# The first block's Down projection as seven block products, with a changed entry and norm around it

## What is computed

```python
# first_block, end
x = x + mix @ w_out[l]
h = rms_norm(x, g_ffn[l])
x = x + (jax.nn.silu(h @ w_gate[l]) * (h @ w_up[l])) @ w_down[l]   # D_FF = 2816
# second_block, start: 16 meta tokens stand ahead of x
u = rms_norm_2(h, g_mix[layer])
z = jnp.einsum('bld,df->blf', u, w_in[layer])
```

## Time and profile before

| | us |
|---|---|
| median of 3 runs | 3392.05 (3387.78 to 3392.68) |
| the profiled execution, device time | 3388.14 |
| its span, first to last instruction | 3386.3 |
| PE busy, PEld busy | 3217.8 (95%), 2841.0 (84%) |
| DVE, ACT, POOL busy | 1649.5 (49%), 1126.6 (33%), 992.5 (29%) |
| mean granted TensorE clock | 0.975 |

### The profile page before, as it was taken

The page is one execution under the profiler, slowest core; times in us unless marked ns, Lnnn a source line. Parts: engine busy times, 40 slices in busy tenths (PEclk is TensorE's granted clock), DMA queues, the critical chain, the costliest instruction groups (busy, mean ns, idle before and its releaser), DMA issues.

```text
span 3386.3 us, 51779 instructions
## 1 busy us (share of the span) xinstructions
PE 3217.8 (95%) x20325; PEld 2841.0 (84%) x20325; DVE 1649.5 (49%) x2795; ACT 1126.6 (33%) x2100; POOL 992.5 (29%) x672
## 2 busy tenths in 40 slices
PE   7999989899999998999999899999999999789997
PEld 5677767688887887999999799998999999679997
DVE  4555556655554545666666723255455044522223
ACT  3433333333322213555555621155455111300002
POOL 3112223787772323222222133200000222012222
PEclk9999999999999998999999999999999999889998
DMA  4011112122234112000000012100000121468988
GB/s 155 26 32 32 32 63 87 63 87 75 81 107 173 45 45 93 20 20 26 20 20 20 14 44 82 65 25 26 23 23 20 69 95 62 175 216 308 318 307 292
DMA packets 80577, 294.90 MB, mean 87 GB/s; under 512 B 11298, under 2 KB 16226, under 8 KB 77200
## 3 DMA queue, kind: packets, MB, share of 16 engines
q1 hardware_dynamic: 69744, 251.92, 21.2%
q0 software_dynamic: 6160, 18.63, 2.2%
q10 hardware_dynamic: 4496, 21.90, 1.6%
HBM read 239.39 MB, written 47.70 MB: 85 GB/s over the span
## 4 chain that ended last, share of the span: by engine, by line
PE 55%; DVE 3%; issue 2%; ACT 1%; DMA 0%; POOL 0%; POOLq 0%; SPq 0%; DVEq 0%; ACTq 0%
PE PS L630 14%; PE PS L3003 7%; PE PS L3425 7%; PE PS L618 5%; PE PS L3188 4%; PE PS L3455 3%; PE PS L3067 3%; PE PS L3034 3%; PE PS L3264 3%; PE PS L3229 2%; PE PS L3068 0%; PE PS L3016 0%; PE PS L3201 0%; DVE where L2855 0%; PE PS L3265 0%
## 5 line engine op out<-in xcount | busy, mean ns | idle before, releaser
L652 POOL CAST w_hi<-ring 128x1024 fp32r<-128x1024 f32 x130 | 137.9, 1061 | 1547.8 <-PE PS L630 436.0
L654 POOL TENSOR_TENSOR w_lo<-ring,w_hi 128x1024 fp32r<-128x1024 f32 x130 | 333.2, 2563 | 10.5
L2142 ACT ACTIVATE EA<-EA,small_sb 128x1040 f32<-128x1040 f32 x144 | 166.8, 1158 | 192.5 <-DVE small_sb L2545 192.2
L2545 DVE CUSTOM_DVE_ANT_0 EA<-PS,biasH,low_a 128x1024 f32<-128x1024 f32 x128 | 163.5, 1278 | 56.4 <-PE PS L3034 56.4
L3003 PE MATMUL PS<-u_hi,w_hi 128*128 128x348 f32 x504 | 173.5, 344 | 0.0
L3003 PE MATMUL PS<-u_lo,w_hi 128*128 128x348 f32 x504 | 162.1, 322 | 0.0
L3003 PE MATMUL PS<-u_hi,w_lo 128*128 128x348 f32 x504 | 161.9, 321 | 0.0
L1563 DVE TENSOR_TENSOR hid_lo<-hid,hid_hi 128x1024 fp32r<-128x1024 f32 x44 | 95.0, 2200 | 121.7 <-ACT hid_hi L1213 121.7
L1647 PE MATMUL PS<-u_hi,w_hi 128*128 128x512 f32 x352 | 147.2, 418 | 3.0 <-POOL w_lo L654 2.3
L630 PE MATMUL PS<-u_hi,w_hi 128*128 128x348 f32 (+1 forms) x552 | 131.2, 342 | 13.1 <-POOL w_lo L654 7.4
L3067 PE MATMUL PS<-Va,PTa 128*128 128x128 f32 (+1 forms) x1152 | 139.9, 275 | 0.0
(11 more groups left out here) (479 smaller groups left out, 8260.2 us busy)
## 6 DMA issues: line engine op xcount, KB each, us to landing
ring<-in_stream SPq DMA_DIRECT2D x130, 512.0 KB, 3.5
w_gate_sb<-in_w_gate SPq DMA_DIRECT2D x64, 512.0 KB, 6.6
w_up_sb<-in_w_up SPq DMA_DIRECT2D x64, 512.0 KB, 7.0
w_down_sb<-in_w_down SPq DMA_DIRECT2D x64, 512.0 KB, 5.7
gu_raw<-in_gate_up SPq DMA_DIRECT2D x22, 1024.0 KB, 5.6
hid_keep<-hid_out SPq DMA_DIRECT2D x17, 512.0 KB, 2.9
hid<-hid_keep SPq DMA_DIRECT2D x17, 512.0 KB, 10.4
x_keep<-xT ACTq DMA_DIRECT2D x1, 4176.0 KB, 13.0
```

The lines of the kernel that those rows point to most:

```text
L652: pool.tensor_copy(w_hi[j][:, :, :], w_raw[j][:, :, :]).then_inc(S["w_rounded"], 1)
L654: pool.tensor_tensor(w_lo[j][:, :, :], w_raw[j][:, :, :], w_hi[j][:, :, :], ALU.subtract).then_inc(S["w_split"], 1)
L2142: act.activation(e[0:m, :], e[0:m, :], ACT.Exp, scale=-1.0, bias=small[0:m, 8 + 2 * par + k:9 + 2 * par + k], accum_out=small[0:m, 12 + 2 ...
L2545: dve.tensor_tensor_reduce(e[0:m, 0:T1], wide(2 * k, T1, m), bias, -1.0, low_a[0:m, t, k:k + 1], ALU.add, ALU.min, low).then_inc(S["aa_max ...
```

## The change

1. **Down by seven block products.** The weights are cut into 2x2 blocks (11 hidden chunks by 4 output chunks), the hidden values into 2x2 blocks (11 hidden chunks by 512 tokens). Seven products s0 to s6 (DP1, DP2, DP7, DP5, DP6, DP3, DP4) of 11 steps each make 77 steps `q`; one step has 4 output chunks x 3 passes = 12 matmuls of 512 columns, 924 in all where there were 1056. In each step ACT rounds the weights (`d_hi`) and the values (`o_hi`), POOL makes `d_lo` and DVE `o_lo`; there are four buffers of each.
2. **Operands made step by step.** The weights' sums: S3 by DVE (for s2), S1, S2, S4 by POOL (for s3, s4, s5), one step ahead. The values' differences T1, T3, T2, T4 by DVE, in steps of s0, s1, s3, s4, written over `hid`. Each product is added to one to four places of `x2T` by DVE in the steps of the next product.
3. **Loads.** Raw blocks of 256 KB come to 12 slots by SP, 99 of them. ACT issues 15 of the 17 reloads of hidden chunks. Chunks 0 and 1 are stored and reloaded, 2 to 5 stay. Early in gate and up, `gu_raw1` waits for two stores and 8 lo parts only; its roundings stand between those of t4.
4. **Norms.** In the entry of gate and up root, reciprocal and diagonal stand earlier, and the spreading stands before A22, in banks 2 and 3. At the end of Down the squares' sums go straight through a 128x128 matrix of ones; root and reciprocal are taken of 128x1044 values in SBUF (`sd2`).
5. **Splits.** The second block's tiles A0 and A0+1 are both split by POOL within Down's last product.

```diff
+KH = NF // 2
+DOWN = (("A11", "B11"), ("A12", "B21"), ("S3", "T3"), ("S1", "T1"), ("S2", "T2"), ("S4", "B22"), ("A22", "T4"))
+RAW_SLOTS = 12
+STEP_SLOTS = 4
+TWIST = 4
+ADDS = (2, 1, 1, 1, 2, 1, 1)
...
         def norm_total(dve, k):
+            if k == 2:
+                for n, cols in enumerate((slice(0, BANK), slice(BANK, TP))):
+                    dve.wait_ge(N["sd"], pieces_upto(1) + n + 1)
+                    dve.reciprocal(sd2[:, cols], sd2[:, cols]).then_inc(N["r"], 2)
+                dve.wait_ge(N["r"], 2 * pieces_upto(2))
+                return
...
-            return dve.scalar_tensor_tensor(dst, src[:, c, 0:width], gains[:, NORM_GAINS[k] + c:NORM_GAINS[k] + c + 1], wide(8 - pieces[k] - 1, width),
+            root = sd2[:, 0:width] if k == 2 else wide(8 - pieces[k] - 1, width)
+            return dve.scalar_tensor_tensor(dst, src[:, c, 0:width], gains[:, NORM_GAINS[k] + c:NORM_GAINS[k] + c + 1], root,
...
@@ SP
-                sp.wait_ge(S["keep_st"], 16 + 16 * KD)
-                sp.wait_ge(S["op_lo"], 7 * HALF)
+                sp.wait_ge(S["x_st"], 32)
+                sp.wait_ge(S["op_lo"], 8)
                 load_pair(1)
...
+                for f in range(STAY.start):
+                    sp.dma_start(hid[:, f, :], hid_keep[:, f, :]).then_inc(S["hid_ld0"], 16)
+                for n in range(4, len(RAWS)):
+                    load_down(n)
...
@@ POOL
+                for q in range(DSTEPS):
+                    if q + 1 < DSTEPS:
+                        combine_down(q + 1)
+                    pool.wait_ge(S["dw_hi"], q + 1)
+                    pool.tensor_tensor(d_lo[q % STEP_SLOTS][:, :], weight_source(q), d_hi[q % STEP_SLOTS][:, :], ALU.subtract).then_inc(S["dw_lo"], 1)
+                    if q == DP4 * KH + 5:
+                        pool.wait_ge(S["dw_lo"], DP4 * KH + 1)
+                        split(pool, A0, 0, A0 // 2 + 1, A0 - 2)
+                    if q == DP4 * KH + 8:
+                        split(pool, A0 + 1, 1, A0 // 2 + 1, A0 - 1)
...
@@ ACT
                 for q in range(HALF):
                     act.wait_ge(S["op_t"], 3 * HALF + 2 * q + 2)
                     round_operand(t4, q, t4_raw[q % 2][:, :])
+                    round_slot(1, (A11, S1, S2, S3)[q])
...
+                load_hid(STAY.stop, 11)
+                act.wait_ge(S["gs_used"], used(NF - 1, S1))
+                load_hid(11, 15)
...
                 act.dma_start(x2T[:, :, :], x_keep).then_inc(S["keep_ld"], 16)
...
+                for q in range(STEP_SLOTS, DSTEPS):
+                    if q == STAY.stop:
+                        act.wait_ge(S["hid_ld"], 16 * (NF - 1 - STAY.stop))
+                    round_weight(q)
+                    round_values(q)
...
+                for n, (cols, sums) in enumerate(((slice(0, BANK), bank(5)), (slice(BANK, TP), wide(6, TP - BANK)))):
+                    act.wait_ge(N["ss"], 4 + n)
+                    act.activation(sd2[:, cols], sums, ACT.Sqrt, scale=1.0 / D, bias=eps[:, :]).then_inc(N["sd"], 1)
...
@@ DVE
-                first_sums(0)
+                norm_recip(dve, 1)
+                for all_tokens in tiles_of(1):
+                    diagonals(dve, sq[0], by_token(1), all_tokens).then_inc(N["r"], 1)
                 for q in range(HALF):
                     lower_operand(b22, q, right(xm, HALF + q), 5 * HALF + q + 1, mix_gain(HALF + q))
-                up_right(0)
+                first_sums(0)
...
+                for k in range(2):
+                    combine_values(DP1, k)
+                dve.wait_ge(S["keep_ld"], 32)
+                for q in range(2, DSTEPS):
+                    s, k = divmod(q, KH)
+                    rest_values(q)
+                    if q + 1 < DSTEPS:
+                        combine_weights(q + 1)
+                    combine_values(s, k)
+                    p, late = divmod(k - 3, 2)
+                    if s and p >= 0 and not late:
+                        add_product(s - 1, p)
...
@@ PE
+                for q in range(DSTEPS - TWIST):
+                    operands_ready(q)
+                    for p in range(HALF):
+                        last = down_step(q // KH, q % KH, p)
+                    last.then_inc(S["dn_used"], 1)
+                operands_ready(DSTEPS - 1)
+                for p in range(HALF):
+                    for k in range(KH - TWIST, KH):
+                        last = down_step(DP4, k, p)
+                last.then_inc(S["dn_used"], 1)
+                pe.wait_ge(N["acc"], 2 * (KD + 1) + CREDIT)
+                mm(bank(5), ones[:, :], acc[:, 0:BANK], start=True, stop=True).then_inc(N["ss"], 1)
+                mm(bank(6), ones[:, :], acc[:, BANK:T1], start=True, stop=True)
+                mm(bank(7, TP - T1), ones[:, :], acc[:, T1:TP], start=True, stop=True).then_inc(N["ss"], 1)
```

More of the change, by code:

```diff
@@ L53 @@
 EVICT = "v s c22 w u1 c11 g0 c12 g1 hid1 c21 u0 hid0".split()
-KEPT = 4
+STAY = range(2, 6)
+KH = NF // 2
+DOWN = (("A11", "B11"), ("A12", "B21"), ("S3", "T3"), ("S1", "T1"), ("S2", "T2"), ("S4", "B22"), ("A22", "T4"))
+DSTEPS = KH * len(DOWN)
+RAW_OF = {"A11": ("A11",), "A12": ("A12",), "A22": ("A22",), "S3": ("A11", "A21"), "S1": ("A21", "A22"), "S2": ("A11",), "S4": ("A12",)}
+RAWS = [(s * KH + k, name, k) for s, (w, _) in enumerate(DOWN) for k in range(KH) for name in RAW_OF[w]]
+RAW_SLOTS = 12
+STEP_SLOTS = 4
+TWIST = 4
+DP1, DP2, DP7, DP5, DP6, DP3, DP4 = range(7)
+ADDS = (2, 1, 1, 1, 2, 1, 1)
 HEADS = 8
@@ L474, in build @@
         S.update(first_sems)
+        dw_lds = [nc.alloc_semaphore(name=f"dw_ld{j}") for j in range(RAW_SLOTS)]
         xin_lds = [sem(f"xin_ld{j}") for j in range(NT)]
@@ L1199, in _ @@
                         take_first(i)
-                    for s in (A11, S1, S2, S3, A12):
+                    for s in (A11, S1, S2, S3, A12) if i else (A12,):
                         round_slot(i + 1, s)
@@ L1206, in _, with load_hid @@
                 take_first(NF - 1)
-                silu_half(NF - 1, 0)
-                def round_tile(m, c):
-                    act.wait_ge(S["w_used"], tile_done(DOWN0 + m - 2))
-                    for k in range(2):
-                        act.activation(hid_hi[2 * slot + k][:, :], hid[:, bass.ds(c + k, 1), :].rearrange("p a n -> p (a n)"), ACT.Copy).then_inc(S["hid_hi"], 1)
+                def load_hid(first, last):
+                    for f in range(first, last):
+                        act.dma_start(hid[:, f, :], hid_keep[:, f, :]).then_inc(S["hid_ld"], 16)
@@ L1538, in _ @@
                     diagonals(dve, sq[0], by_token(1), all_tokens).then_inc(N["r"], 1)
+                for q in range(HALF):
+                    lower_operand(b22, q, right(xm, HALF + q), 5 * HALF + q + 1, mix_gain(HALF + q))
+                first_sums(0)
+                dve.wait_ge(S["gs_used"], used(0, S3))
+                evict(0, "s", c21[:, :], product_bank(0, S3), v_sum[:, :], ALU.add, "v")
                 for q in range(HALF):
@@ new lines, in down_step @@
+                def down_step(s, k, p):
+                    j = (s * KH + k) % STEP_SLOTS
+                    if k == 0:
+                        if s == 0 and p:
+                            pe.wait_ge(S["gs_out"], out_of(NF - 1, "w"))
+                        if s >= 2:
+                            pe.wait_ge(S["dn_ev"], added(s - 2, p))
+                    for q, (w, src) in enumerate(((d_hi, o_hi), (d_hi, o_lo), (d_lo, o_hi))):
+                        last = mm(down_bank(s, p), w[j][:, p * P:(p + 1) * P], src[j][:, :], start=(k == 0 and q == 0), stop=(k == KH - 1 and q == 2))
+                    if k == KH - 1 and p < HALF - 1:
+                        last.then_inc(S["dn_p"], 1)
+                    return last
@@ L3509, in layout @@
     late += [*w_in2[GB:GB + KD], *w_b, *w_out2]
-    out["stream"] = np.concatenate([np.stack(tiles), down, np.stack(late)])
+    out["stream"] = np.concatenate([np.stack(tiles), np.stack(late)])
     for n in ("w_gate_2", "w_up_2"):
```

341 lines of the change are left out of this document (199 added, 142 removed).

## The result

The changed kernel is slower: 3406.83 us in the median (3404.97 to 3407.66) where the kernel before has 3392.05 (five runs of each, the latter 3386.54 to 3392.68); the ratio is 1.0048, with a 95% interval of 1.0034 to 1.0061. The prediction was 3387.3 with a range of 3370 to 3403, so the time lies above the range, on the side that I held less likely.

The account below looks back on a forecast made before the run. Matmuls times their distance plus PE's holes bound gate and up and Down; -7.5 (entry), +1.2 (Down) and +1.5 (norm) make -4.8 us on the profiled 3388.1, and with 3.9 for the median 3387.3, range 3370 to 3403.

Parts of the forecast that it names:

- What bounds the kernel: In gate and up and Down, time is matmuls times their distance, 0.2267 us each in Down, plus PE's holes.
- PE's own work: Down falls from 1056 to 924 matmuls, 29.9 us less; one step of 12 is 2.72 us.
- The arrival of x2T: Down's start: DVE's rest of step 2 waits for x2T until 1046; a hole of some 17 us, 1.65 of slow clock.
- DVE and POOL exclude each other: Down's steps: turns cost 3.42 us per step in s3 and s4, 2.96 in s5; together 13.2 us, bounds 5 and 20.
- s2 has the same with S3 in place of a difference: Down's s2: one POOL and two DVE instructions per step, 2.2 us, under PE's 2.72.
- the three steps ahead are used up first: Down's s3 and s4: the lead is spent before PE lags, so step 54's operands are 10.6 us late.
- Down's end: Before the last four steps: POOL's split brings 3.3 us of waiting, perhaps a low clock; 3.9 us, bounds 2 and 6.
- The entry: Entry of gate and up: the second hole goes, the second chunk starts at 608.5; -7.5 us, bounds -5 and -10.
- A22 still ends at about 608.5: Entry of gate and up: DVE gets to t4 at about 599.4, 599.6 before, so A22's end stays at about 608.5.
- The norm: After Down: -0.8 earlier product, +6.5 for reading SBUF, -3.5 for the early split, -0.7 low clock; +1.5 us, bounds -3 and +5.
- The rivals: Whole kernel: faster one 3373, chance 0.28; slower one 3398 or 3402, 0.27; one below 3355, 3 in 100.
- B, the slower one: Down's s3 and s4: steps cost 3.9 us instead of 3.42, +10.6, 3398, or 3402 with a falling clock; chance 0.27.

Follow-up runs that it names:

- all edits: The changed kernel with the six edits, the old norm, S1, S2 and S4 summed by DVE, and TWIST = 2: 3349.79 us, ratio 0.9878.
- TWIST = 2: The kernel with the six edits and the old norm, only Down's last 2 steps, not 4, run output chunk by output chunk: 3358.62 us.
- the six edits: Changed kernel with x2T waited for at step 14, S3 ahead of the rest, A0+1 split later, chunk 1 roundings behind t4, two reorderings at Down's start: 3367.55 us.

## Why the prediction was wrong

**What bounds the kernel, and PE's own work** were right: 12 matmuls take 2.72 us wherever PE is fed, and with all edits Down is 30.6 us shorter than before. That this is so near to 29.9 is chance: it still has 6.1 us of waiting and slow clock, and Down before had 6.8.

**The arrival of x2T.** Right: the wait, what is queued behind it, and that it costs about 20 us. The term was mis-sized by 3.1 us. I took 1046 as the landing, 21.8 us after the issue, out of a sum of 15.8 MB; it took 24.5. The step that failed is "as the raw blocks are on the other queue", by which I left out the up to 1.6 MB of six more raw blocks: 14 had been issued and 17.35 MB moved by the landing, which is the upper end, 1050, of my own sum. The slow clock held twelve matmuls and not eight, 2.6 us for 1.65. I had found the price of a wait that stands 12 steps ahead of its need, and did not ask more of it.

**DVE and POOL exclude each other.** The size was right for the turns: 3.41 us for 3.42 in s3 and s4, 2.95 for 2.96 in s5. The step that failed is "s2 has the same with S3 in place of a difference", that is under 2.72 us. It counted how long each engine is busy and not the path from one step's sum through ACT's two roundings and the rest to the next sum: 3.24 us. That cost 4.5 us in s2, and 4.6 more in s3 and s4, because "the three steps ahead are used up first" presumed a lead that this path doesn't allow. With the path cut the measured lag was 10.3, with 10.6 forecast.

**Down's end.** The stop was placed right, at the right matmul and with POOL's split in it. 3.9 us were forecast and 8.1 measured, 6.4 of stop and 1.5 of slow clock. The step that failed is that the wait was put down to POOL's split alone. The split took 4.7 us in place of 3.4 (beside DVE), and without it 3.5 us of stop stay, with 1.5 to 2.9 of slow clock behind them. These come from the twist: with TWIST = 2 both are gone. I had taken the clock at half of 1.3.

**The entry.** The step that failed is "A22 still ends at about 608.5". I kept t4's pace of the kernel before, but the change puts POOL's work for chunk 1 beside it, and the rule that I had just worked out for Down, DVE 1.66 for 0.75 beside POOL, was not applied here. The moved stop came back as three (1.4, 4.0, 3.4 us). With ACT's order mended, the gain against the kernel before is 38.3 - 32.0 = 6.2 us, inside the bounds of -5 to -10.

**The norm.** The +6.5 us for the products that read SBUF were about right: the whole old norm in the new one's place gives 6.7 us (5.5 on top of the six edits). The -0.7 us for the clock was too small: before, tile A0+1 ran at a granted clock of 0.81 and took 15.9 us, now at 1.00 and 13.1. Windows of before, then of after, PE alone:

```profile
1305.30:1321.20 15.90, 14.48 (x72) 0.81 0.22 68
```

```profile
1327.70:1340.80 13.10, 11.68 (x73) 1.00 0.39 126
```

So that stage came out at -1.0 for +1.5.

**The rivals.** None came as told. B, the slower one, had the right sign for a wrong reason: it asked for 3.9 us a step, and 3.41 was measured; the time that it lacked lay in places where I saw no wait at all. My five errors of +3.1, +4.5, +4.6, +4.2 and +7.1 us make 23.5; the norm (-2.5) and s5 (-0.4) went the other way, so Down and the changed stages as a whole are 21 us off, and the medians 19.5. Each of the five is something else that waits once the first wait is gone, and my bounds for Down (5 to 20, 2 to 6) and the entry (-5 to -10) did not hold a case in which one engine's new work lengthens another's old work.

## What to carry to other kernels

A producer that runs on three engines has two limits: how long each engine is busy per step, and how long one round takes from an operand to the next one that is queued behind it on the same engine. Work out both; here they were 3.41 and 3.25 us, and moving POOL's sums to DVE brought nothing as long as the second stood, and 11.1 us of Down once it was cut. A lead hides a pace that is too slow for as long as it lasts, so look at how it shrinks. When a change starts an engine earlier, go through what runs beside it at that time, first of all DVE instructions with two SBUF inputs beside POOL. A wait belongs to the instruction that needs it: placed twelve steps early it cost 17 us, more than the whole loss of this change.
